# adaLN products in four column groups of the array, and weight splits moved behind them on two engines

## What is computed

```python
mod = jax.nn.silu(c) @ ada_w + ada_b             # c: 1 prompt row + 8 sequence rows, ada_w 1024 x 3072
shift, scale, gate = jnp.split(mod, 3, axis=-1)
hn = (_rmsnorm(x, pre_w) * (1.0 + scale[:, None]) + shift[:, None]).astype(x.dtype)
z = hn @ w_in                                    # w_in 1024 x 3072
...
x = x + (gate[:, None] * _rmsnorm(m, post_w)).astype(x.dtype)
```

## Time and profile before

| | us |
|---|---|
| three runs | 1023.69, 1025.93, 1023.05 |
| median | 1023.69 |
| span of the profiled execution (no other time of it is given) | 1026.3 |
| TensorE busy in it | 984.2 |
| DVE, ACT busy in it | 582.0, 430.0 |

### The profile page before, as it was taken

The page is one execution under the profiler, slowest core; times in us unless marked ns, Lnnn a source line. Parts: engine busy times, 40 slices in busy tenths (PEclk is TensorE's granted clock), DMA queues, the critical chain, the costliest instruction groups (busy, mean ns, idle before and its releaser), DMA issues.

```text
span 1026.3 us, 19994 instructions
## 1 busy us (share of the span) xinstructions
PE 984.2 (96%) x7423; PEld 714.3 (70%) x7478; DVE 582.0 (57%) x1652; ACT 430.0 (42%) x810; POOL 161.0 (16%) x208
## 2 busy tenths in 40 slices
PE   7899986899999999999999999999999999999987
PEld 3465875469775887579766976697759775887554
DVE  1453688436763576436754566366635773477445
ACT  2531747313651365135713373237413661345321
POOL 4000024301130112011110112011301130111212
PEclk9999998899999999999999999999999999999998
DMA  9984301100110011000110011001101010100413
GB/s 313 326 275 130 118 24 59 62 2 21 42 63 0 20 41 43 19 20 0 42 62 0 21 41 62 0 21 41 62 0 41 0 50 1 42 1 23 118 42 111
DMA packets 46590, 60.62 MB, mean 59 GB/s; under 512 B 2748, under 2 KB 40208, under 8 KB 46524
## 3 DMA queue, kind: packets, MB, share of 16 engines
q1 hardware_dynamic: 46524, 59.86, 17.8%
HBM read 48.90 MB, written 10.95 MB: 58 GB/s over the span
## 4 chain that ended last, share of the span: by engine, by line
PE 90%; DVE 5%; issue 2%; ACT 1%; DMA 1%; SPq 1%; DVEq 0%; ACTq 0%
PE ring L390 66%; PE lev L464 7%; PE aux L507 3%; PE okv L521 2%; PE lev L469 1%; PE okv L491 1%; PE lev L462 1%; PE ring L521 1%; PE okv L493 1%; PE okv L492 1%; DMA work<-in_w_in_dram 1%; PE okv L811 1%; PE aux L441 1%; PE aux L477 1%; PE aux L428 1%
## 5 line engine op out<-in xcount | busy, mean ns | idle before, releaser
L390 PE MATMUL ring<-hnh,wih 128*128 128x256 bf16 (+1 forms) x1152 | 291.1, 264 | 5.8 <-DVE hnl L1273 4.2
L390 PE MATMUL ring<-hnh,wil 128*128 128x256 bf16 (+1 forms) x1152 | 291.2, 264 | 0.0
L390 PE MATMUL ring<-hnl,wih 128*128 128x256 f16 (+1 forms) x1152 | 291.1, 264 | 0.0
L390 PE MATMUL ring<-woh,work 128*128 128x512 f16 x512 | 162.3, 379 | 1.7
L390 PEld LDWEIGHTS ring<-hnh,wih 128*128 128x128 f16 x1152 | 112.5, 100 | 18.1 <-issue 4.5
L1165 DVE TENSOR_TENSOR qq<-qq,gg 128x256 f32<-128x256 f32 x96 | 44.1, 459 | 140.1 <-PE lev L464 99.8
L390 PEld LDWEIGHTS ring<-hnl,wih 128*128 128x128 f16 x1152 | 110.6, 98 | 12.9
L390 PEld LDWEIGHTS ring<-hnh,wil 128*128 128x128 bf16 x1152 | 110.6, 98 | 12.4
L390 PE MATMUL ring<-wih,hnh 128*128 128x512 f16 (+1 forms) x264 | 101.1, 383 | 4.0 <-ACT kk L851 4.0
L390 PE MATMUL ring<-wih,hnl 128*128 128x512 f16 (+1 forms) x264 | 101.1, 383 | 1.4 <-issue 0.2
L1587 POOL TENSOR_TENSOR kk<-kk,cols 128x256 f32<-128x256 f32 x32 | 29.3, 935 | 419.3 <-ACT kk L851 419.3
(11 more groups left out here) (310 smaller groups left out, 1585.5 us busy)
## 6 DMA issues: line engine op xcount, KB each, us to landing
xin<-in_x_prompt_dram SPq DMA_DIRECT2D x16, 512.0 KB, 3.4
work<-in_x_prompt_dram SPq DMA_DIRECT2D x16, 512.0 KB, 4.3
out_dram<-work SPq DMA_DIRECT2D x16, 512.0 KB, 2.6
work<-in_ada_w_dram SPq DMA_DIRECT2D x4, 1024.0 KB, 10.4
woh<-in_ada_w_dram SPq DMA_DIRECT2D x4, 1024.0 KB, 11.8
work<-in_w_in_dram SPq DMA_DIRECT2D x4, 1024.0 KB, 7.2
woh<-in_w_in_dram SPq DMA_DIRECT2D x4, 1024.0 KB, 8.5
wol<-in_w_in_dram SPq DMA_DIRECT2D x4, 1024.0 KB, 9.6
```

The lines of the kernel that those rows point to most:

```text
L390: last = mm(out, a(k), b(k), start=start and k == ks[0] and j == 0, stop=stop and k == ks[-1] and j == 2)
```

## The change

`siluc` is padded from 9 to 32 columns per chunk (`AW`), with zeros that DVE writes at the very start; ACT's Silu waits for that. Each matmul of 9 rows by 256 columns becomes two of 32 rows by 128 columns, whose outputs go to different strips of 32 partitions of the bank: piece i uses strips 2 (i mod 2) and 2 (i mod 2) + 1. A pair of pieces thus fills 128 partitions x 128 columns of a bank. `mod_out` copies 128 x 128, `turn_mod` is one 128 x 128 transpose, and DVE picks the nine columns out of each 32 (`by_chunk`). On ACT, mod_out(3) goes ahead of convert 0, and convert 1 goes behind hn. On DVE, subtract 0 goes behind the mod instructions and subtract 1 behind the rest part of hn.

```diff
+AW = 32
...
+        pad_zero = sem("pad_zero")
...
+        siluc = xc[:, 0, 0:KT * AW].rearrange("p (k s) -> p k s", k=KT)
+
+        def by_chunk(t, n):
+            return t[:, 0:n * AW].rearrange("p (k s) -> p k s", s=AW)[:, :, 0:NS]
...
@@ TensorE: ada
-                o = 256 * (i % 2)
                 for k in range(KT):
-                    last = mm(bank[0:NS, o:o + 256], siluc[:, k, :], w[:, k, :], start=k == 0, stop=k == KT - 1)
+                    for e in range(2):
+                        o = AW * (2 * (i % 2) + e)
+                        last = mm(bank[o:o + AW, 0:P], siluc[:, k, :], w[:, k, P * e:P * e + P],
+                                  start=k == 0, stop=k == KT - 1)
                 last.then_inc(ada_ps, 1)
@@ TensorE: turn_mod
-                for j in range(4):
-                    last = nc.tensor.transpose(bank[:, o + NS * j:o + NS * j + NS], mod_rows[b][0:NS, P * j:P * j + P],
-                                               ident[0:NS, 0:NS])
-                last.then_inc(mod_ps, 1)
+                nc.tensor.transpose(bank[:, o:o + P], mod_rows[b][:, 0:P], ident[:, :]).then_inc(mod_ps, 1)
@@ ACT: mod_out
-                A(mod_rows[b][0:NS, :], bank[0:NS, :], ACT.Copy).then_inc(mod_sb, 1)
+                A(mod_rows[b][:, 0:P], bank[:, 0:P], ACT.Copy).then_inc(mod_sb, 1)
@@ ACT: prologue
             act.wait_ge(pre_ps, 1)
-            A(xc[:, 0, 0:KT * NS], aux[1][:, 0:KT * NS], ACT.Silu).then_inc(pre_sb, 1)
+            act.wait_ge(pad_zero, 1)
+            A(siluc[:, :, 0:NS], aux[1][:, 0:KT * NS].rearrange("p (k s) -> p k s", k=KT), ACT.Silu).then_inc(pre_sb, 1)
...
             mod_out(2, lev[0])
+            mod_out(3, lev[1])
             head("wi", 0)
-            mod_out(3, lev[1])
-            head("wi", 1)
             act.wait_ge(mod_ok, 1)
             for j in range(4):
                 hn_out(0, j)
+            head("wi", 1)
             head("wi", 2)
@@ DVE: body 0, and prologue
-                    gate = aux[0][:, 0:KT * NS].rearrange("p (k s) -> p k s", s=NS)
+                    gate = by_chunk(aux[0], KT)
...
+            V.memset(siluc, 0.0).then_inc(pad_zero, 1)
             dve.wait_ge(pre_sb, 2)
...
             x_norm(0)
-            rest(0)
 
             dve.wait_ge(mod_ps, 4)
...
-            mod = ring[0][:, 0:2 * KT * NS].rearrange("p (k s) -> p k s", s=NS)
+            mod = by_chunk(ring[0], 2 * KT)
...
-            rest(1)
+            rest(0)
             for j in range(4):
                 hn_rest(0, j)
+            rest(1)
             rest(2)
```

## The result

The changed kernel takes 1032.08 us in the median of four runs (1030.73 to 1034.19), the kernel before 1024.7 in the median of four on the same chip (1023.05 to 1025.93). The ratio is 1.0069, with a 95% interval of 1.0049 to 1.0088. By that estimate the profiled execution of the kernel before (span 1026.3) took 1028.0 us, 3.3 more than its median: the two traces lie 3.2 us apart where the medians lie 7.4 apart.

What follows compares the result with a forecast made beforehand. The prediction took TensorE, busy 96% of the span, as the bound, with the weight stream and ACT pacing the prologue. Savings of 4.5 (prologue) and 7.0 (body 0) made 11.5 us: 1023.7 - 11.5 = 1012.2 us, range 1010 to 1019.5.

Steps and rivals of the forecast that it cites:

- body 0: Four last adaLN pieces on TensorE's path fall from 3.55 to 1.8 us each, saving 7.0 us, with followers hidden.
- Price of a piece: One adaLN piece on TensorE in column groups: 1.8 us, with strips overlapping and the doubled weight loads costing nothing.
- The rule of the Trainium skill on weight loads and row groups: Loads overlap matmuls in flight only in other row groups; by it a piece takes 3.6 us, no gain.
- Prologue: Up to TensorE's first projection: hn on ACT starts at 37.42 instead of 41.95 us, saving 4.5 us.
- each early piece waits for its load: In the prologue, from piece 1's end each piece waits for its load; the last runs 31.74 to 33.5 us.
- The wait on the subtract of block 1: TensorE's second projection waits for DVE's subtract of block 1 in the prologue: 0 to 0.2 us.
- the hidden memset: DVE's new memset of the padding, awaited by ACT's Silu at the start: costs nothing, 0.5 us without cover.
- the queue of loads: The SP queue waits for block 1's subtract before loading piece 9; 2 us of cover are left.
- Rivals: Three alternatives: no overlap (1021.7 us, 0.10), body 0 gives its part back (1019.2, 0.10), weight loads exposed (near 1064, 0.05).
- The slower one: Rival: each of 32 records waits for its weight load, 7.1 us a piece, time near 1064 us; chance 0.05.
- Body 0 gave nothing back: Judges the rival that something else in body 0 ends last, leaving only the prologue's 4.5: 1019.2 us; chance 0.10.
- The chance of 0.05 for slower: Probability of a slower kernel, given only to weight loads coming into the open on TensorE.

Runs made afterwards that it cites:

- e2: The kernel before with 92 more filler instructions on TensorE ahead of the loop, giving it the changed kernel's place: 1042.39 us, ratio 1.0151.
- e4: The kernel before with only the moves on ACT and DVE: 1023.67 us, ratio 0.9978 to the kernel before.
- e5: e3 without the moves on ACT and DVE, so column groups from piece 2 on: 1019.32 us, ratio 0.9930 to the kernel before.
- e1: The changed kernel with 164 filler instructions on TensorE ahead of the loop, restoring its place of before: 1017.13 us, ratio 0.9913 to the kernel before.
- e3: The changed kernel with pieces 0 and 1 in the old form, without filler: 1015.54 us, ratio 0.9889 to the kernel before.
- e10: e1 with 8 fewer filler instructions, so the loop starts 8 instructions ahead of its place of before: 1050.17 us in one run.

## Why the prediction was wrong

The step that failed is the last sentence on body 0: "From there on all waits are between engines, so the whole shift of 11.5 us is carried to the end." It left out a resource: the store that TensorE's own program is read from. I had counted records and weight loads per piece, 32 in place of 16, and cost the loads at nothing beside the matmuls; that they are also instructions ahead of a loop I did not count. The trace of before could have told it: q8's packets come one by one up to 269.5 us and from 830.8 us, and not at all while the loop turns. A resource that is quiet for that long holds the whole loop; how near the edge was, that trace doesn't say. e2 puts the price of the missed term at 16 us in the kernel before (15.4 of it in the loop), and in the trace of the changed kernel it took 15.9 us from a lead of 13.7.

**Price of a piece**: right. 1.8 us forecast, 1.74 to 1.87 measured. Alternate strips overlap at 128 columns, and twice as many weight loads stay hidden: 32 of 110 ns each, one after the other, would take 3.5 us.
The rule of the Trainium skill on weight loads and row groups (TensorE: Matmul & The Clock Gate, Part 3, The mechanism), set against it in the prediction, does not hold for these products: all use 128 rows, and at the 3.6 us that the prediction works out by it a piece would have gained nothing.

**Prologue**: right. 4.5 us forecast; hn 4.84 us earlier, TensorE's first projection 4.83, of which 0.3 is an earlier landing of block 0. That the moves need the groups is shown by e4 and e5: 2.3 us alone, 4.2 on top of the groups. That each early piece waits for its load did not hold for 6 and 7, which the slow piece 5 made late; the last ended at 33.70, and 33.5 was forecast. The wait on the subtract of block 1, the hidden memset and the queue of loads held.

**Body 0**: right, and a little short. 11.1 us at the second unit's successor against 11.5; e5, the groups without the moves, gains 7.2 where 7.0 were forecast. Of the further 2.6 us of lead at the loop 1.7 are the projection at 98.25, which lasts 5.41 us and not 7.08 (granted 1.00 from 98.3 to 101.0 us, before 0.55 from 109.4 to 112.0). But e4 has the old pieces and the same hole ahead of that projection (1.4 us), and there it is granted 1.00 too:

```profile
107.92 5.41 PE ring L390 x48
```

So these 1.7 us are no gain of the change: the profiled execution of the kernel before lost them there, and another with the same pieces did not. By the estimate above up to 3.3 us of the lead of 13.7 belong to that execution; what the rest of the 2.6 is stays open. It fits that e1 and e3, which I had expected to gain 13.7, gained 9.0 and 10.6 by the medians.

**Rivals**: none held. The slower one needed weight loads in the open, and they are hidden. Body 0 gave nothing back. The chance of 0.05 for slower was put on one mechanism and should have covered the code itself.

With the loop's place set right, the forecast is met: e3 gains 1.1% of 1026.17, 11.4 us by the ratio (10.6 by the medians), where 11.5 were forecast.

## What to carry to other kernels

Where an engine runs a long loop, count the instructions that a change adds ahead of it on that engine, and look at the instruction queues of the profile before and after: packets in a stretch where the loop turns mean that its code is fetched again. An edit of a few instructions outside a loop can cost more than it earns, and the same few put elsewhere give it back; when a trace is ahead up to a loop and then loses the same amount at each turn, test the loop's place with filler before doubting the edit.

## What the runs showed of the hardware that I had not expected

A loop of 1717 instructions on TensorE stays loaded over six passes when it starts in the right 75 or so of 256 places, and is read again on each pass otherwise, nine packets of 16 KB. In the changed kernel a turn then costs a hole of 2.0 to 2.4 us, and behind three of the five a lower clock (0.53 to 0.66 granted in 3.6 us); with a boundary 8 instructions behind the loop's start it costs two holes, 33 us over five turns (e10).
The Trainium skill (Runtime: NRT & Kernel Launch, Instruction fetch mechanics) says that TensorE holds 128 KiB of instructions, 2048, refilled in 16 KiB blocks of 256, and that a taken branch whose target is not in the current window of two pages waits for a transfer. The packets of 16 KB and the holes agree. The window of two pages (512 instructions) does not: by it the loop would wait at every turn wherever it stands, and in the kernel before no packet came from 269.5 to 830.8 us. Nor is the size alone the limit: the runs show a loop of fewer than 2048 instructions that is too long by where it begins.

Two matmuls in different column strips start 7 ns apart and run together, also in f32 and with 128 columns each. The low clock of TensorE behind the hole before 25.60 cost nothing at hn, since the products still ended ahead of the landing of block 0: ACT has copied the last pair by 34.03 us and then waits for that load until 35.30.
